# Mixing and experts in one block: first expert's weights split beside the shared output, last scores ahead of shared down, three store buffers

## The chip, the cores and the metric

The kernel runs on one core of a Trainium2 chip, as one program with one launch. The time is device time in microseconds (us); the figure that is compared is the median of a few runs. A core has TensorE (PE; its weight loads are shown as PEld), VectorE (DVE), ScalarE (ACT), GpSimd (POOL) and SyncE (SP). Each engine works through its own list in order and waits on semaphores for the others. SyncE and GpSimd also issue transfers (DMA), SyncE plain ones, GpSimd those whose rows are picked by an index.

## What is computed

One layer of a streaming encoder for 512 prompt tokens and 32 tokens of a running stream, all in f32, 1024 wide:

```
proj = x @ w_in                                 # q, k, v, z, gates, lx, ly
o    = gated_delta_rule(conv(q,k,v)) * silu(z)  # 8 heads of 128, in chunks
lru  = rg_lru(conv(lx)) * gelu(ly)
h1   = layer_norm(alpha * x + [o | lru] @ w_out)
scores = sigmoid(h1 @ router_w)                 # 64 experts in 8 groups
idx  = the 8 best experts of the 4 best groups; gw = their scores / sum * 2.5
shared = (silu(h1 @ sh_w_gate) * (h1 @ sh_w_up)) @ sh_w_down
routed = sum_j gw[j] * (silu(h1 @ w_gate[idx_j]) * (h1 @ w_up[idx_j])) @ w_down[idx_j]
y    = layer_norm(alpha * h1 + shared + routed)
```

## The kernel before

Five stages follow each other, each in a block of its own: `projection_stage`, `delta_rule_stage`, `mixing_stage`, `expert_stage`, `combine_stage`. A block ends with a barrier: each engine drains, that is, waits until what it has issued has ended, and none goes on before all have arrived. The order of the work inside a block is written out by hand for each engine. The change touches the third and the fourth stage.

`mixing_stage` multiplies by `w_out` (`mix`), turns the result to rows (`turn_mixed`), adds the residual and normalises (`normalise` on VectorE gives `h1`), turns `h1` back (`turn_h1`, copied out of PSUM by ScalarE's `copy_h1`) and computes the router's scores (`score`, L1378). The tokens come in five tiles in the order 2, 3, 4, 0, 1 (`ORDER`); tile 4 holds the 32 stream tokens. For each tile VectorE's `choose` (L1559 to L1592) finds the eight experts and writes a table of ones, `chosen` (L1585). TensorE's `ranks` (L1388) counts from it how many earlier tokens an expert has, VectorE's `place` (L1599 to L1602) turns this into a place in the list of entries, and GpSimd then writes the tile's entries there, by eight indexed transfers (L1694). When all are in memory, GpSimd reads the list of the 64 experts back (`slot_ids`, L1699) and issues the gathers of `h1` rows for the first three experts (L1183). Beside this runs the shared expert: `shared_up` (L1405, four passes of two parts), `gate` on ScalarE, `shared_hidden` on VectorE (L1621), `shared_down` for each tile (L1420), and `add_shared` on VectorE (L1631), after which SyncE stores the tile to `residual_rows`. `list_extra` and `extra_rows` (L1434) prepare a list of extra blocks for experts with over 128 tokens. SyncE has loaded the weights of the first three experts (3 MB each) since 779 us.

`expert_stage` takes the 64 experts one by one. Weights and gathered rows are split in two parts of lower precision: ScalarE writes the high part (`gate_up_hi`, L1936; `rows_hi`, L1945), VectorE the rest (`gate_up_lo`, L1993; `rows_lo`, L2002), each expert's weights in two halves. TensorE turns the rows (L1851), does 24 matmuls of gate and up (L1864 to L1866), turns the next expert's rows, does the down product of the expert before (L1884) and turns the hidden values. `write_y` on ScalarE (L1952) and VectorE (L2009) writes the weighted result to one of two buffers `y`, and GpSimd scatters them to `expert_rows` (L1802). Before `write_y(b)` both engines wait until the scatter of expert b - 2 has landed. At the stage's start ScalarE does, in this order:

```
for b in range(2):
    for u in range(2):
        split(b, u)
    if b == 0:
        read_rows(0)
```

and VectorE the same with its own parts. TensorE's first expert matmul needs `split(0, 0)` and `read_rows(0)` of both.

Of the kernel before, what the change touches and what calls it, by code (L numbers as in the profile page):

```python
# [18 lines left out]
F32 = mybir.dt.float32  # L19
BF16 = mybir.dt.bfloat16  # L20
# [1147 lines left out]
RAW = 3  # L1168
ROWS = 3
# [57 lines left out]
def mixing_stage(nc, mem, dram, route, spent):  # L1227

    with ExitStack() as ctx:  # L1229
        def sem(name):  # L1230
            return ctx.enter_context(nc.semaphore(name))

        C, PR = mem.consts, mem.params
        carve = mem.carve
        zt = carve(mem.zt, 0, DC, TW)
        lru = carve(mem.lru, 0, DC, TW)
        w_out = carve(mem.wide, 0, DC, 2 * DC, P)
        n_work = 22912
        work = mem.sbuf(ctx, "mixing_work", n_work)
        at = 0  # L1240

        def take(*dims):
            nonlocal at
            view = carve(work, at, *dims)
            at += int(np.prod(dims))
            return view

        w_gu, w_dn, w_router, ln = take(DC, 2 * FF), take(FC, D), take(DC, NE), take(2, D)
        h1 = [take(D) for _ in range(TILES + 1)]
        h1_t = take(DC, TW)  # L1250
        mixed = h1_t
        act_g, hidden_t = [take(TW - 2 * P) for _ in range(2)], take(FC, TW)
        stats, biased, masked = take(32), take(NE), take(NE)
        scores = [take(NE) for _ in range(2)]
        best, group, group_best, group_f = take(NG, 8), take(NG), take(NG), take(NG)
        group_i, top_i = take(8).bitcast(U32), take(8).bitcast(U32)
        group_eq, group_on, penalty, top_v, total = take(NG, TOPG), take(NG), take(NG), take(8), take(2)
        expert, weight, rank = take(TOPK), take(TOPK), take(TOPK)
        hot, hot_s = take(TOPK, NE), take(TOPK, NE)
        entry_f = take(TILES + 1, TOPK, 4)  # L1260
        entry = entry_f.bitcast(U32)
        dest = take(TILES + 1, TOPK).bitcast(U32)
        assert at <= n_work

        before_b, ones_b = (ctx.enter_context(nc.sbuf_tensor(n, [P, P], BF16)) for n in ("before_bf16", "ones_bf16"))

        s_w = [sem(f"w_out_loaded_{i}") for i in range(4)]
        s_sh, s_ln = sem("shared_loaded"), sem("norm_loaded")
        s_x = [sem(f"x_loaded_{t}") for t in range(TILES + 1)]
        s_copied, s_turned = sem("mix_copied"), sem("mix_turned")  # L1270
        s_mix, s_x1, s_h1, s_ht, s_htr = sem("mixed"), sem("mix_read"), sem("h1_ready"), sem("h1_transposed"), sem("h1_t_ready")
        s_scored, s_sc, s_gu, s_g, s_hid = (sem("scores_ready"), sem("scores_read"), sem("shared_up"),
                                            sem("shared_gate_ready"), sem("shared_hidden"))
        s_dn, s_acc = sem("shared_down"), sem("residual_ready")
        s_h1out = [sem(f"h1_stored_{t}") for t in range(TILES + 1)]
        s_accout = sem("residual_stored")
        s_sel, s_rank, s_placed, s_count = sem("chosen_ready"), sem("ranks_ready"), sem("entries_placed"), sem("experts_counted")
        s_extra, s_extra_row, s_v = sem("extra_blocks"), sem("extra_blocks_rows"), sem("mix_vector_steps")
        s_listed, s_ids = sem("entries_listed"), sem("slot_ids_loaded")
        block = ctx.enter_context(nc.Block())  # L1280
        tiles = token_tiles()

        def columns(t):

            return slice(tiles[t][1], tiles[t][1] + tiles[t][2])

        def group_columns(g):

            return slice(2 * P, TW - 1) if g == 0 else slice(0, 2 * P)

        def down_pair(i):

            return (4, 0, 4, 2, 0)[i]

        @block.sync
        def _(sp):
            def load_x(t):
                w = tiles[t][2]
                sp.dma_start(h1[t][0:w], dram["x_rows"][P * t:P * t + w, :]).then_inc(s_x[t], 16)

            for i, (a, b) in enumerate(zip(W_OUT_PARTS, W_OUT_PARTS[1:])):
                sp.dma_start(w_out[:, a:b], dram["w_out"][:, a:b]).then_inc(s_w[i], 16)
            load_x(ORDER[0])
            sp.dma_start(ln, dram["norms"][:, 0:2, :]).then_inc(s_ln, 16)
            sp.dma_start(w_router, dram["w_router"]).then_inc(s_sh, 16)
            load_x(ORDER[1])
            n_gu = DC * 2 * FF
            sp.dma_start(w_gu, dram["w_sh"][:, 0:n_gu].rearrange("p (k n) -> p k n", k=DC)).then_inc(s_sh, 16)
            sp.dma_start(w_dn, dram["w_sh"][:, n_gu:].rearrange("p (k n) -> p k n", k=FC)).then_inc(s_sh, 16)
            for t in ORDER[2:]:  # L1310
                load_x(t)
            def store_h1(i):
                t, w = ORDER[i], tiles[ORDER[i]][2]
                sp.wait_ge(s_h1, i + 1)
                sp.dma_start(dram["h1"][P * t:P * t + w, :], h1[t][0:w]).then_inc(s_h1out[t], 16)

            for i in range(len(GROUPS[0])):
                store_h1(i)
            sp.wait_ge(s_mix, 2 * DC)
            for b in range(RAW):  # L1320
                load_expert(sp, mem, dram, b)
            for i in range(len(GROUPS[0]), TILES + 1):
                store_h1(i)
            for i, t in enumerate(ORDER):
                w = tiles[t][2]
                sp.wait_ge(s_acc, i + 1)
                sp.dma_start(dram["residual"][P * t:P * t + w, :], h1[t][0:w]).then_inc(s_accout, 16)
            sp.wait_ge(s_accout, 16 * (TILES + 1))

        @block.tensor  # L1330
        def _(pe):
            def mix(g, d, fs):

                n, cols = DC * g + d, group_columns(g)
                if fs[0] == 0:
                    if n >= 2:
                        pe.wait_ge(s_copied, n - 1)
                    if g == 0 and d in W_OUT_PARTS:
                        pe.wait_ge(s_w[W_OUT_PARTS.index(d)], 16)
                for f in fs:  # L1340
                    last = nc.tensor.matmul(mem.bank[d % 2][:, 0:cols.stop - cols.start], w_out[:, d, f, :],
                                            (zt if f < DC else lru)[:, f % DC, cols],
                                            start=(f == 0), stop=(f == 2 * DC - 1))
                if fs[-1] == 2 * DC - 1:
                    last.then_inc(s_mix, 1)

            def turn_mixed(i):

                t, w = ORDER[i], tiles[ORDER[i]][2]
                pe.wait_ge(s_copied, DC if t in GROUPS[0] else 2 * DC)  # L1350
                if i:
                    pe.wait_ge(s_x1, i)
# [951 lines left out]
```

## Time and profile before

| | us |
|---|---|
| median of 3 runs | 1609.47 |
| lowest and highest | 1601.35, 1614.27 |
| the profiled execution: time | 1609.28 |
| its span, first to last instruction | 1607.5 |
| projection and delta rule | 0 to 646 |
| mixing, to TensorE's last matmul | 646 to 845.5 |
| first to last matmul of the experts | 864.6 to 1509.9 |
| combine | to 1607.5 |
| busy: TensorE, VectorE, ScalarE, GpSimd | 1468.6, 1009.9, 606.1, 348.8 |
| TensorE's mean granted clock | 0.952 |

The profile shows one execution. Positions in it are us from the span's start. The granted clock is a share of TensorE's full 2.4 GHz; 0.50 is its lower level, 1.2 GHz. Busy time is without semaphore, branch and DMA-issuing instructions.

### The profile page before, as it was taken

Reading aid. Unit: us, or ns where it says so; the run is one execution under the profiler, and the core shown is the slowest. Engines: PE = TensorE matmul, PEld = TensorE weight load, DVE = VectorE, ACT = ScalarE, POOL = GpSimd, SP = SyncE. Lnnn points to the kernel's source line nnn. Section 1 sums busy time; section 2 is a strip of 40 time slices with the busy share of each in tenths; the row PEclk is TensorE's granted clock in tenths of the full one; section 3 lists DMA queues with packets and bytes.
Section 4 is the critical chain, followed back from the end, with each engine's and each line's share of the span. In section 5 each row is a group of like instructions: output and inputs, shape, how many; then the busy total and the mean of one; then the engine's idle time right before and its main releaser. Section 6 shows DMA issues by size and latency. Waiting matters only on the chain. (4 is left out here: it accounts for less than half of the span.)

```text
span 1607.5 us, 21220 instructions
## 1 busy us (share of the span) xinstructions
PE 1468.6 (91%) x8256; PEld 1174.6 (73%) x8260; DVE 1009.9 (63%) x1712; ACT 606.1 (38%) x890; POOL 348.8 (22%) x233
## 2 busy tenths in 40 slices
PE   7999999979999986899995999999999999999564
PEld 5999999968888875688753667777777777777321
DVE  5649877235657665018665777777777777777277
ACT  2575333340330320001104555555555555556101
POOL 0000000022223312001441333333333223221124
PEclk9999999979999996899997999999999999999886
DMA  5212222200000000900515999999999999997392
GB/s 204 68 66 93 85 86 91 68 14 1 1 1 1 1 1 27 376 1 31 232 65 192 370 367 377 369 377 370 369 367 362 367 369 365 361 370 296 137 401 95
DMA packets 53305, 313.25 MB, mean 195 GB/s; under 512 B 14944, under 2 KB 15968, under 8 KB 34336
## 3 DMA queue, kind: packets, MB, share of 16 engines
q1 hardware_dynamic: 33456, 276.16, 45.4%
q0 software_dynamic: 19760, 35.89, 6.0%
q8 instruction: 57, 0.93, 0.2%
q14 instruction: 32, 0.26, 0.0%
HBM read 301.33 MB, written 42.12 MB: 214 GB/s over the span
## 5 line engine op out<-in xcount | busy, mean ns | idle before, releaser
L1993 DVE TENSOR_TENSOR gate_up_lo<-wide,gate_up_hi 128x2048 fp32r<-128x2048 f32 x128 | 293.0, 2290 | 101.1 <-ACT gate_up_hi L1936 99.5
L1936 ACT ACTIVATE gate_up_hi<-wide 128x2048 fp32r<-128x2048 f32 x128 | 244.6, 1913 | 29.6 <-PEq L1229 29.6
L310 PE MATMUL bank<-x_hi,w_hi 128*128 128x274 f32 x768 | 223.9, 291 | 0.0
L312 PE MATMUL bank<-x_hi,w_lo 128*128 128x274 f32 x768 | 223.0, 290 | 0.0
L311 PE MATMUL bank<-x_lo,w_hi 128*128 128x274 f32 x768 | 222.0, 289 | 0.0
L1864 PE MATMUL bank<-gate_up_hi,rows_hi 128*128 128x512 f32 x512 | 206.2, 403 | 7.1 <-DVE rows_lo L2002 7.1
L1866 PE MATMUL bank<-gate_up_hi,rows_lo 128*128 128x512 f32 x512 | 201.2, 393 | 0.0
L1865 PE MATMUL bank<-gate_up_lo,rows_hi 128*128 128x512 f32 x512 | 200.5, 392 | 0.0
L1802 POOL DMA_INDIRECT expert_rows<-lru,slot_ids x64 | 129.3, 2021 | 311.7 <-DVE lru L2009 299.3
L1884 PE MATMUL bank<-wide,zt 128*128 128x512 f32 x344 | 154.8, 593 | 1.0 <-DVE zt L2029 1.0
L310 PEld LDWEIGHTS bank<-x_hi,w_hi 128*128 128x128 f32 x768 | 144.9, 189 | 0.8 <-issue 0.5
L311 PEld LDWEIGHTS bank<-x_lo,w_hi 128*128 128x128 f32 x768 | 145.0, 189 | 0.3
L312 PEld LDWEIGHTS bank<-x_hi,w_lo 128*128 128x128 f32 x768 | 145.0, 189 | 0.0
L1864 PEld LDWEIGHTS bank<-gate_up_hi,rows_hi 128*128 128x128 f32 x512 | 96.6, 189 | 26.2 <-DVE rows_lo L2002 7.7
L1866 PEld LDWEIGHTS bank<-gate_up_hi,rows_lo 128*128 128x128 f32 x512 | 96.5, 188 | 21.1
L1865 PEld LDWEIGHTS bank<-gate_up_lo,rows_hi 128*128 128x128 f32 x512 | 96.8, 189 | 18.8
L1884 PEld LDWEIGHTS bank<-wide,zt 128*128 128x128 f32 x344 | 62.0, 190 | 62.9 <-issue 61.7
L1964 ACT ACTIVATE zt<-bank 128x256 f32<-128x256 f32 x64 | 24.6, 385 | 215.7 <-PE bank L1866 215.7
L1183 POOL DMA_INDIRECT zt<-h_rows,slot_ids x64 | 66.5, 1039 | 161.5 <-PE bank L1851 154.8
L494 DVE TENSOR_TENSOR w_lo<-w_raw,w_hi 128x1024 fp32r<-128x1024 f32 x48 | 58.7, 1224 | 56.0 <-ACT w_hi L385 54.9
L2002 DVE TENSOR_TENSOR rows_lo<-bank,rows_hi 128x512 fp32r<-128x512 f32 x128 | 82.4, 686 | 17.1 <-ACT rows_hi L1945 16.8
L991 POOL TENSOR_TENSOR delta_work<-consts,decay 128x1024 f32<-128x1024 f32 (+1 forms) x5 | 8.9, 1785 | 330.2 <-POOLq L193 330.2
(280 smaller groups left out, 2475.6 us busy)
## 6 DMA issues: line engine op xcount, KB each, us to landing
wide<-in_w_exp SPq DMA_DIRECT2D x64, 2048.0 KB
wide<-in_w_exp SPq DMA_DIRECT2D x43, 1024.0 KB
w_raw<-in_w_in SPq DMA_DIRECT2D x48, 512.0 KB, 3.5
last_down<-in_w_exp SPq DMA_DIRECT2D x21, 1024.0 KB
expert_rows<-expert_rows SPq DMA_DIRECT2D x8, 2048.0 KB, 13.5
wide<-in_w_out SPq DMA_DIRECT2D x1, 4096.0 KB, 22.0
zt<-in_x_t SPq DMA_DIRECT2D x2, 1096.0 KB, 9.3
wide<-in_w_out SPq DMA_DIRECT2D x2, 1024.0 KB, 5.9
```

Source lines behind the costliest of these rows:

```text
L310: nc.tensor.matmul(out, wh[:, k, :], x_hi[:, k, at], start=(k == 0), stop=False)
L311: nc.tensor.matmul(out, wh[:, k, :], x_lo[:, k, at], start=False, stop=False)
L312: last = nc.tensor.matmul(out, wl[:, k, :], x_hi[:, k, at], start=False, stop=(k == DC - 1))
L1183: return pool.indirect_dma_start(out=into, out_offset=None, in_=dram["h1"], in_offset=bass.IndirectOffsetOnAxis(ap=index, axis=0), bounds_ ...
L1802: return pool.indirect_dma_start(out=dram["expert_rows"], out_offset=bass.IndirectOffsetOnAxis(ap=index, axis=0), in_=source, in_offset=No ...
L1864: nc.tensor.matmul(out, x_hi[i][:, k, :], w_hi[i][:, at], start=(k == 0), stop=False)
L1865: nc.tensor.matmul(out, x_hi[i][:, k, :], w_lo[i][:, at], start=False, stop=False)
L1866: last = nc.tensor.matmul(out, x_lo[i][:, k, :], w_hi[i][:, at], start=False, stop=(k == DC - 1))
L1884: last = nc.tensor.matmul(mem.bank[4 + n][:, :], hidden_t[:, c, :], w_dn[b % RAW][:, c, 512 * n:512 * n + 512], start=(c == 0), stop=(c == ...
L1936: nc.scalar.activation(half(w_hi[b % 2], u), half(w_gu[b % RAW], u), ACT.Copy).then_inc(s_whi, 1)
L1993: nc.vector.tensor_tensor(half(w_lo[b % 2], u), half(w_gu[b % RAW], u), half(w_hi[b % 2], u), ALU.subtract).then_inc(s_wlo, 1)
L2002: nc.vector.tensor_tensor(x_lo[b % 2][:, at, :], in_fours(mem.bank[h]), x_hi[b % 2][:, at, :], ALU.subtract).then_inc(s_xlo, 1)
```

## The change

Both stages now stand in one block. Each returns one function per engine, and `mixing_and_experts` runs, on each engine, the mixing part and then the expert part, with no barrier between. What the barrier guarded is now guarded by waits: TensorE waits for the last `add_shared` before its first expert matmul, ScalarE (before its first silu) and VectorE (before its low half of expert 1's weights) wait for all residual stores. The memory of mixing is laid out so that the first expert's split weights fall on the shared gate and up weights, `h1_t` and `ln`. The first expert's weights are split in quarters, by ScalarE at the end of its mixing part and by VectorE between the last `add_shared` steps. `shared_down(0)` moves behind all `shared_up`, so that the last scores come before it, and VectorE does `place(3)` before `shared_hidden(1)` and `add_shared(0)` after `list_extra`. Three buffers `y` instead of two. Of ScalarE's and VectorE's alike changes the diff shows ScalarE's; VectorE has `split_rows(0)`, its wait, and then its halves of `split(1, u)`. The function with the five numbers is `down_pair`, the first PSUM bank of each tile's shared down.

```
+Y_ROWS = 3
 ...
-            w_gu, w_dn, w_router, ln = take(DC, 2 * FF), take(FC, D), take(DC, NE), take(2, D)
-            h1 = [take(D) for _ in range(TILES + 1)]
-            h1_t = take(DC, TW)
+    w_gu, h1_t, ln = take(DC, 2 * FF), take(DC, TW), take(2, D)
+    w_dn, w_router = take(FC, D), take(DC, NE)
 ...
+    h1 = [take(D) for _ in range(TILES + 1)]
 ...
-            return (4, 0, 4, 2, 0)[i]
+        return (4, 0, 4, 2, 4)[i]
 ...
-            sp.wait_ge(s_accout, 16 * (TILES + 1))
 ...
             turn_h1(4)
-            shared_down(0)
             score(4)
             ranks(3)
 ...
             shared_up(3, 1)
-            for i in range(1, TILES + 1):
+        for i in range(TILES + 1):
                 shared_down(i)
 ...
             gate(3)
+        act.wait_ge(s_gu, 4 * FC)
+        for q in range(4):
+            split_first(q)
 ...
             choose(3)
+        place(3)
             shared_hidden(1)
-            place(3)
             choose(4)
             shared_hidden(2)
             place(4)
-            add_shared(0)
             list_extra()
             shared_hidden(3)
-            for i in range(1, TILES + 1):
+        for i in range(TILES + 1):
                 add_shared(i)
+            if i < TILES:
+                split_first(i)
 ...
+    def split_first_hi(q):
+        if q == 0:
+            nc.scalar.wait_ge(s_gu_w[0], 16)
+        nc.scalar.activation(quarter(w_hi[0], q), quarter(w_gu[0], q), ACT.Copy).then_inc(s_whi, 1)
+
+    def split_first_lo(q):
+        nc.vector.wait_ge(s_whi, q + 1)
+        nc.vector.tensor_tensor(quarter(w_lo[0], q), quarter(w_gu[0], q), quarter(w_hi[0], q),
+                                ALU.subtract).then_inc(s_wlo, 1)
 ...
             transpose_rows(0)
+        pe.wait_ge(s_mixed_read, TILES + 1)
 ...
-            for b in range(2):
-                for u in range(2):
-                    split(b, u)
-                if b == 0:
-                    read_rows(0)
+        read_rows(0)
+        for u in range(2):
+            split(1, u)
+        act.wait_ge(s_mixed_stored, 16 * (TILES + 1))
 ...
-                if b >= 2:
-                    act.wait_ge(s_out[b % 2], 16 * (b // 2))
+            if b >= Y_ROWS:
+                act.wait_ge(s_out[b % Y_ROWS], 16 * (b // Y_ROWS))
 ...
-            mixing_stage(nc, mem, dram, route, spent)
-            expert_stage(nc, mem, dram, route)
+            mixing_and_experts(nc, mem, dram, route, spent)
```

TensorE's list from the last turn of `h1` (bank4, bank5) to the first `shared_up` of the second group, before:

```order
L1365 MATMUL bank4<-consts,mixing_work 128x128 [waits h1_t_ready,h1_ready]
L1365 MATMUL bank4<-consts,mixing_work 128x128 x3
L1365 MATMUL bank5<-consts,mixing_work 128x128 x4
L1420 MATMUL bank4<-mixing_work 128x512 [waits h1_t_ready,shared_hidden]
L1420 MATMUL bank4<-mixing_work 128x512
L1420 MATMUL bank5<-mixing_work 128x512 x2
L1378 MATMUL bank6<-mixing_work 128x64 [waits h1_t_ready,scores_read]
L1378 MATMUL bank6<-mixing_work 128x64 x7
L1388 MATMUL bank7<-chosen,ones_bf16 128x64 [waits entries_placed,chosen_ready]
L1388 MATMUL bank7<-chosen,ones_bf16 128x64 x2
L1388 MATMUL bank7<-chosen,before_bf16 128x64
L1405 MATMUL bank0<-mixing_work 128x256 [waits h1_t_ready,shared_hidden]
```

and now:

```order
L1361 MATMUL bank4<-consts,mixing_work 128x128 [waits h1_t_ready,h1_ready]
L1361 MATMUL bank4<-consts,mixing_work 128x128 x3
L1361 MATMUL bank5<-consts,mixing_work 128x128 x4
L1374 MATMUL bank6<-mixing_work 128x64 [waits h1_t_ready,scores_read]
L1374 MATMUL bank6<-mixing_work 128x64 x7
L1384 MATMUL bank7<-chosen,ones_bf16 128x64 [waits entries_placed,chosen_ready]
L1384 MATMUL bank7<-chosen,ones_bf16 128x64 x2
L1384 MATMUL bank7<-chosen,before_bf16 128x64
L1401 MATMUL bank0<-mixing_work 128x256 [waits h1_t_ready,shared_hidden]
```

The four matmuls of the first `shared_down`, into bank4 and bank5, are gone from here, and with them the wait for `shared_hidden` ahead of the scores in bank6.

TensorE's list from the last `shared_down` to the first expert's matmuls, before (`zt` holds the gathered rows):

```order
L1420 MATMUL bank0<-mixing_work 128x512 [waits residual_ready,shared_hidden]
L1420 MATMUL bank0<-mixing_work 128x512
L1420 MATMUL bank1<-mixing_work 128x512 x2
L1229 UNCONDITIONAL_BRANCH
L1840 UNCONDITIONAL_BRANCH [waits barrier_Pool_Activation_PE_DVE_SP_release]
L1851 MATMUL bank0<-consts,zt 128x128 [waits rows_gathered_0]
L1851 MATMUL bank0<-consts,zt 128x128 x3
L1851 MATMUL bank1<-consts,zt 128x128 x4
```

and now:

```order
L1416 MATMUL bank4<-mixing_work 128x512 [waits residual_ready,shared_hidden]
L1416 MATMUL bank4<-mixing_work 128x512
L1416 MATMUL bank5<-mixing_work 128x512 x2
L1866 MATMUL bank0<-consts,zt 128x128 [waits rows_gathered_0]
L1866 MATMUL bank0<-consts,zt 128x128 x3
L1866 MATMUL bank1<-consts,zt 128x128 x4
L1881 MATMUL bank2<-gate_up_hi0,rows_hi0 128x512 [waits weights_lo_ready,row_halves_lo_ready,residual_ready]
L1882 MATMUL bank2<-gate_up_lo0,rows_hi0 128x512
```

The two branches with the barrier are gone; the first turn waits for the gathered rows alone, and the wait for `residual_ready` stands at the first expert matmul.

VectorE's list from the fourth `add_shared` (out of bank2 and bank3) to the first low halves of expert 1, before:

```order
L1631 SCALAR_TENSOR_TENSOR mixing_work<-mixing_work,bank2 128x512 [waits h1_stored_0,shared_down]
L1631 SCALAR_TENSOR_TENSOR mixing_work<-mixing_work,bank3 128x512
L1631 SCALAR_TENSOR_TENSOR mixing_work<-mixing_work,bank0 128x512 [waits h1_stored_1,shared_down]
L1631 SCALAR_TENSOR_TENSOR mixing_work<-mixing_work,bank1 128x512
L1683 CAST routing<-bank7 1x128 [waits extra_blocks_rows]
L1684 CAST routing<-bank7 1x128
L1229 UNCONDITIONAL_BRANCH
L1987 UNCONDITIONAL_BRANCH [waits barrier_Pool_Activation_PE_DVE_SP_release]
L1993 TENSOR_TENSOR gate_up_lo0<-wide,gate_up_hi0 128x2048 [waits weights_hi_ready] x2
L2002 TENSOR_TENSOR rows_lo0<-bank0,rows_hi0 128x512 [waits row_halves_hi_ready]
L2002 TENSOR_TENSOR rows_lo0<-bank1,rows_hi0 128x512 [waits row_halves_hi_ready]
L1993 TENSOR_TENSOR gate_up_lo1<-wide,gate_up_hi1 128x2048 [waits weights_hi_ready] x2
```

and now, from the quarter ahead of the fourth `add_shared` on:

```order
L1789 TENSOR_TENSOR gate_up_lo0<-wide,gate_up_hi0 128x1024 [waits weights_hi_ready]
L1627 SCALAR_TENSOR_TENSOR mixing_work<-mixing_work,bank2 128x512 [waits h1_stored_0,shared_down]
L1627 SCALAR_TENSOR_TENSOR mixing_work<-mixing_work,bank3 128x512
L1789 TENSOR_TENSOR gate_up_lo0<-wide,gate_up_hi0 128x1024 [waits weights_hi_ready]
L1627 SCALAR_TENSOR_TENSOR mixing_work<-mixing_work,bank4 128x512 [waits h1_stored_1,shared_down]
L1627 SCALAR_TENSOR_TENSOR mixing_work<-mixing_work,bank5 128x512
L1680 CAST routing<-bank7 1x128 [waits extra_blocks_rows]
L1681 CAST routing<-bank7 1x128
L2017 TENSOR_TENSOR rows_lo0<-bank0,rows_hi0 128x512 [waits row_halves_hi_ready]
L2017 TENSOR_TENSOR rows_lo0<-bank1,rows_hi0 128x512 [waits row_halves_hi_ready]
L2008 TENSOR_TENSOR gate_up_lo1<-wide,gate_up_hi1 128x2048 [waits weights_hi_ready,residual_stored]
L2008 TENSOR_TENSOR gate_up_lo1<-wide,gate_up_hi1 128x2048 [waits weights_hi_ready]
```

The weights' low quarters (128x1024) stand between the adds, the low halves of the rows come directly after mixing, and the first low half of expert 1 waits for `residual_stored`.

## Rows read from the trace of the kernel before

**Rows 1.** Busy time by stretches: us, each engine (count), clock, DMA share, GB/s.

```profile
846.00:865.00 19.00, 2.37 (x9) 2.00 (x10) 7.37 (x9) 8.12 (x6) 5.69 (x4) 0.54 0.33 102
...
885.00:1100.00 215.00, 215.00 (x903) 151.28 (x902) 155.16 (x151) 119.70 (x127) 77.03 (x43) 1.00 0.97 373
```

**Rows 2.** One operation of VectorE, once per expert: durations ns, first and last start.

```profile
L2021 DVE TENSOR_TENSOR zt<-zt,bank x64: 413/422/422, 872.4 to 1502.0; 128x256 f32<-128x256 f32 x64
```

**Rows 3.** Timeline from the barrier's opening; columns: start, us, what, [idle before <-releaser].

```profile
856.62 1.94 PE L1851 MATMUL bank<-consts,zt 128*128 128x128 f32 x8 [11.14 <-PEq L1229]
...
856.88 3.71 ACT L1936 ACTIVATE gate_up_hi<-wide 128x2048 fp32r<-128x2048 f32 x2 [29.58 <-PEq L1229]
...
860.50 1.07 ACT L1945 ACTIVATE rows_hi<-bank 128x512 fp32r<-128x512 f32 x2
...
863.24 1.28 DVE L2002 TENSOR_TENSOR rows_lo<-bank,rows_hi 128x512 fp32r<-128x512 f32 x2
...
864.57 0.79 PE L1864 MATMUL bank<-gate_up_hi,rows_hi 128*128 128x512 f32 x1 [6.01 <-DVE rows_lo L2002]
```

**Rows 4.** One line's instructions: drains that end the mixing block, ns and start us.

```profile
L1229 POOLq DRAIN  x1: 8456/8456/8456, 847.9 to 847.9; - x1
...
L1229 SPq DRAIN  x1: 7/7/7, 849.6 to 849.6; - x1
```

**Rows 5.** Timeline of the last scatters, the last shared down and the first gather.

```profile
831.45 0.97 POOL L1694 DMA_INDIRECT slot_table<-mixing_work  x1 [2.30 <-DVE mixing_work L1602]
...
841.25 0.60 PE L1434 MATMUL bank<-consts,routing 128*1 128x128 f32 x4
...
841.78 3.70 PE L1420 MATMUL bank<-mixing_work 128*128 128x512 f32 x8
...
842.80 0.60 POOL L1699 DMA_DIRECT2D slot_ids<-slot_table  x1 [1.43 <-DMA slot_table<-mixing_work]
...
845.52 1.28 DVE L1631 SCALAR_TENSOR_TENSOR mixing_work<-mixing_work,bank 128x512 f32<-128x512 f32 x2 [2.87 <-PE bank L1420]
...
847.05 1.06 POOL L1183 DMA_INDIRECT zt<-h_rows,slot_ids  x1 [3.66 <-DMA slot_ids<-slot_table]
```

**Rows 6.** Timeline from three passes of shared up to the last placing.

```profile
816.27 10.61 PE L1405 MATMUL bank<-mixing_work 128*128 128x256 f32 x48
...
818.13 0.20 DVE L1559 TENSOR_SCALAR mixing_work<-mixing_work 128x64 f32<-128x64 f32 x1
...
824.27 0.20 DVE L1585 CAST chosen<-mixing_work 128x64 bf16<-128x64 f32 x1
...
829.04 0.69 DVE L1599 TENSOR_TENSOR mixing_work<-mixing_work,bank 128x512 f32<-128x512 f32 x1 [2.00 <-remote]
...
830.49 0.17 DVE L1602 SCALAR_TENSOR_TENSOR mixing_work<-mixing_work 128x8 uint32<-128x8 f32 x1
```

**Rows 7.** DMA queue of the gathers, 848.5 to 851: packets, MB, share.

```profile
q0 software_dynamic: 150, 0.34, 55.1%
```

**Rows 8.** Timeline before the last scores.

```profile
805.25 1.08 ACT L1502 ACTIVATE mixing_work<-bank 128x512 f32<-128x512 f32 x2 [4.62 <-PE bank L1365]
...
808.68 0.46 DVE L1621 TENSOR_TENSOR mixing_work<-mixing_work,bank 128x291 f32<-128x291 f32 x1
...
809.19 5.40 PE L1420 MATMUL bank<-mixing_work 128*128 128x512 f32 x8 [3.98 <-DVE mixing_work L1621]
...
814.43 1.89 PE L1378 MATMUL bank<-mixing_work 128*128 128x64 f32 x16
```

**Rows 9.** The page's group of the weights' low halves.

```profile
L1993 DVE TENSOR_TENSOR gate_up_lo<-wide,gate_up_hi 128x2048 fp32r<-128x2048 f32 x128 | 293.0, 2290 | 101.1 <-ACT gate_up_hi L1936 99.5
```

**Rows 10.** Timeline of a scatter that started inside an operation of VectorE.

```profile
794.30 1.28 DVE L1216 SCALAR_TENSOR_TENSOR mixing_work<-mixing_work 128x1024 f32<-128x1024 f32 x1
...
794.57 1.76 POOL L1694 DMA_INDIRECT slot_table<-mixing_work  x1 [0.30 <-issue]
```

**Rows 11.** Waits of 864 to 1515 us: total us, times, longest us.

```profile
ACT lru L1952 <- DMA expert_rows<-lru,slot_ids: 56.9, 35, 2.8
```

More of the change, by code:

```diff
@@ L1301, in _ @@
[L1301 to L1308, printed above, removed]
@@ L1320, in _ @@
[L1320 to L1327, printed above, removed]
-            sp.wait_ge(s_accout, 16 * (TILES + 1))
+            mixing["sync"](sp)
+            experts["sync"](sp)
@@ L1330, in _ @@
         @block.tensor
         def _(pe):
[L1332 to L1345, printed above, removed]
@@ L1472, in _ @@
-            shared_up(1, 1)
-            turn_h1(4)
-            shared_down(0)
-            score(4)
-            ranks(3)
-            shared_up(2, 0)
-            shared_up(2, 1)
-            shared_up(3, 0)
-            ranks(4)
-            count()
-            shared_up(3, 1)
-            for i in range(1, TILES + 1):
-                shared_down(i)
-                if i == 3:
-                    extra_rows()
+            mixing["tensor"](pe)
+            experts["tensor"](pe)
         @block.scalar
@@ L1540, in _ @@
-            copy_h1(4)
-            scored(4)
-            gate(2)
-            gate(3)
+            mixing["scalar"](act, experts["first_hi"])
+            experts["scalar"](act)
         @block.vector
         def _(dve):
-            steps = Steps(dve, s_v)
-            nc.vector.tensor_copy(before_b[:, :], C("before"))
-            nc.vector.tensor_copy(ones_b[:, :], C("ones"))
-            steps.link(nc.vector.memset(route.chosen, 0.0))
-            steps.link(nc.vector.tensor_copy(entry.rearrange("p t j c -> p (t j c)"), C("entries")))
@@ L1606, in normalise @@
-            def normalise(i):
-                t, w = ORDER[i], tiles[ORDER[i]][2]
-                dve.wait_ge(s_x[t], 16)
-                dve.wait_ge(s_turned, i + 1)
-                for n in range(2):
-                    half = h1[t][0:w, 512 * n:512 * n + 512]
-                    last = nc.vector.scalar_tensor_tensor(half, half, ALPHA, mem.bank[2 + n][0:w, :], ALU.mult, ALU.add)
-                last.then_inc(s_x1, 1)
-                dve.wait_ge(s_x1, i + 1)
-                layer_norm(nc, steps, h1[t][0:w], stats[0:w], ln[0:w, 0, :], ln[0:w, 1, :]).then_inc(s_h1, 1)
@@ L1678, in _ @@
[L1678 to L1684 removed]
+            mixing["vector"](dve, experts["first_lo"])
+            experts["vector"](dve)
         @block.gpsimd
         def _(pool):
[L1688 removed]
@@ L2049, in combine_stage @@
+            mixing["gpsimd"](pool)
+            experts["gpsimd"](pool)
 def combine_stage(nc, mem, dram, route):
```

1344 lines of the change are left out of this document (710 added, 634 removed).

## The prediction

> **What bounds the kernel now.** I read first the busy table by stretches [rows 1]. From 885 us on TensorE is busy 215.00 of 215 us, at a granted clock of 1.00: the expert loop is TensorE's. Its 64 experts follow each other evenly; the first multiply of gate and up starts at 872.4 and the last at 1502.0 [rows 2], so one expert takes (1502.0 - 872.4) / 63 = 9.99 us. No wait of TensorE stands in the list of waits of that loop. Time can be had only where TensorE is idle, and the stretch 846 to 865 is that place: 2.37 us busy in 19.00, clock 0.54 [rows 1].
>
> I then read the timeline of that stretch backwards, from TensorE's first expert matmul at 864.57 [rows 3]. It waited for the low half of the gathered rows (VectorE, 863.24), this for their high half (ScalarE, 860.50), and this stood behind 3.71 us of splitting the first weights, which began at 856.88, although the weights had long been in memory. Everything begins at 856.6, when the barrier between the two blocks opens. The engines' drain rows [rows 4] say who was late: SyncE arrived at 849.6, while GpSimd's drain of 8.456 us ran from 847.9 to 856.4. So GpSimd closes the block, after it has issued the three first gathers. What leads to them [rows 5]: the list entries of the last token tile are placed at 830.49 + 0.17 = 830.66 [rows 6], eight scatters run 831.45 to 841.37, the list is read back (842.80), the first gather starts at 847.05. Its rows were there about 850.9: by 851 the gathers had moved 150 packets [rows 7], a little more than the 128 rows of the first one.
>
> **The change, part by part.**
>
> (a) The last scores go ahead of shared down. Today TensorE ends the last turn of h1 at 805.21, then waits 3.98 us for shared_hidden(1), which VectorE gives only after choose(3), and then does the eight matmuls of shared_down(0) in 5.40 us; the same eight take 3.70 at full clock, so the idling cost 1.7 more. The last scores come at 814.43 [rows 8]. Afterwards they need only ScalarE's copy, done at 806.33: they start about 806.4, end at 808.2, and the ranks of tile 3 follow, whose choice is on hand before 806.7. VectorE, free at 808.64 (808.68 is its next start), places tile 3 at once: 1.62 us (829.04 to 830.66, [rows 6]), to 810.35; with shared_hidden(1), 0.46, it is at 810.9. choose(4) now starts there and not at 818.13. Its chosen table comes 6.34 us later (818.13 to 824.47), at 817.2, and its end (one 512-wide product and one sum of 0.69 each, three small steps) about 2.1 after that, 819.3. TensorE's three shared_up passes take 10.6 us from 808.3 [rows 6], to 818.8: they, not VectorE, release the last ranks, at 819.0. shared_hidden(2) and place(4) take 0.45 + 1.62: entries placed at 821.4 instead of 830.66, **9.2 us earlier**. GpSimd's backlog doesn't eat this: tile 3 is placed 810.35, its eight scatters take 0.8 + 9.9 us as the last tile's do now, to 821.0.
>
> (b) TensorE's own end of mixing. After the ranks: shared_up(3,1), 3.5, to 822.5; five shared_down of 3.43 each (8 matmuls at 0.43) and 0.54 for the extra rows (841.25 to 841.78, [rows 5]) give 840.2, against 841.78 + 3.70 = 845.5 now. VectorE's last add follows to 841.5. So TensorE is free 5 us earlier and no longer the later of the two.
>
> (c) The first weights' splits move under shared down. 3.71 us of ScalarE and 4.5 of VectorE leave the entrance. ScalarE has been idle there for 29.6 us [rows 3], so its four quarters (3.71 us in all) cost nothing. VectorE's quarters (half of 2290 ns, 1.15 us each, [rows 9]) lie between add_shared steps: one add takes 1.28, one shared_down 3.43, which leaves 1.0 us; if that cover were gone each would delay the next add. But GpSimd issues its scatters at the same time. When a scatter started at 794.57 inside VectorE's 1.28 us operation on two operands of mixing_work, it took 1.76 us [rows 10] where others take 0.97 [rows 5]; it ended 0.75 after VectorE did. A quarter of 1.15 against scatters every 1.28 catches nearly always one start, and delays it by 0 to 1.15, on average 0.5. The first quarter can start at 822.5 + 3.43 + 1.28 = 827.2, the next each one shared_down later. Two quarters (827.2, 830.6) fall into the scatters of the last tile, a third (834.1) on the list's read-back, the fourth (837.5) ends before the gather: 0.5 + 0.5 + 0.4 = **1.4 us lost**, ends 0 and 3.5. [...]
>
> (d) The barrier goes. First gather: placed 821.4, + 0.8 to GpSimd's start, + 9.9 for eight scatters [rows 5], + 1.4 (c), + 1.43 until the entries have landed, + 4.25 (842.80 to 847.05) = 839.2; rows about 3.85 after the start (847.05 to 850.9) = 843.0. TensorE, free since 840.2, turns them. From the turn's start to the first expert matmul: 1.94 for both halves at half clock, ScalarE's second half 0.54, VectorE's 0.64, hand-overs 0.1 = 3.2 us. First matmul at 846.2 instead of 864.57: **18.4 us saved**. I take half clock, since TensorE idles 2.8 us beforehand and the 3.98 us of today brought it down.
>
> (e) New waits. Before the second expert's low weights VectorE waits for all residual stores. Behind this are queued the split of expert 1 and the first hidden product. The last store is issued at 841.6 and landed in some 2.4 us in the trace (SyncE is at its drain 849.6 after the add's end at 846.8 [rows 4, 5]): 844.2, before VectorE has finished the rows (846.1). The split ends about 850.9, its first half by 848.6, while TensorE needs that first half at about 854 (8 us after its first matmul). Zero, with 5 us of cover. ScalarE's same wait stands before its first silu, at 853: zero. TensorE's wait for the last add (841.5): zero.
>
> (f) Three store buffers. ScalarE waits in the loop 35 times, 56.9 us in all, for the store of two experts ago [rows 11]. It had spare time: 119.70 busy in 215 us, and TensorE was at 215.00 of 215. Zero; bounds +1 and -1 us.
>
> Sum against the profiled execution: 1609.28 - 18.4 = 1590.9 us. That execution lies 0.2 us under the median of the three runs, 1609.47, so the forecast is **1591 us**.
>
> **Rivals.**
> 1. A late slot. TensorE idles 1.2 us before the moved scores (805.2 to 806.4). If its clock falls there, three shared_up passes lose some 1.7 us as shared_down(0) did [rows 8], the last ranks and all behind them come as much later; if each quarter holds a scatter in full besides, 2.1 more. 18.4 - 3.8 = 14.6: 1594.9. For it: the clock did fall in this neighbourhood. Against: after a gap three times as long.
> 2. All falls well: no scatter is held (1.4), and after an idle time of only 1.4 us TensorE keeps its clock, which gives the turn 0.9 less and the first expert 1.7 less. 22.4: 1587.1.
> 3. Something not in the trace (code that has to be fetched, a store or gather that lands late among the new loads) takes 6 to 13 us of the entrance back: about 1600. Then the new wait for the stores (e) is the last one; it decides from a landing 5 us later than I have.
> 4. **Slower.** The third buffer lets ScalarE run ahead, splits end up to 2.8 us earlier and weight loads are issued earlier, among the stores. DMA is at 0.97 from 885 to 1100 [rows 1]. If loads and gathers get in each other's way until TensorE waits for weights, the loop's period rises; the gain is gone at 18.4 / 63 = 0.29 us more per expert, and at 0.8 more (10.8 us) the kernel takes 1591 + 50 = 1641. For it: 0.97, and the 35 waits for stores. Against: the same bytes in the same time, and from 885 to 1100 TensorE never waited.
> 5. The change doesn't do what it says: GpSimd's gathers would still stand behind a barrier. The order shows none, so I give it nothing.
>
> **How the numbers follow.** Forecast (saving 16 to 20.5) 0.55; rival 1 0.20; rival 2 0.16; rival 3 0.06; rival 4 0.03. Savings of 14 to 22.5 us hold 0.9 of this and are 1587 to 1595.5; runs of the kernel before lie 8.1 under and 4.8 over their median, so a median of a few runs may stand 4 to 5 off: 1582 to 1600. A measurement of this kernel can tell about 1%, 16.1 us, from no change: the line is 1593.4, only 2.4 over the forecast. The whole forecast case and rival 2 lie under it, but the scatter of runs takes some of it away: faster 0.61, within 1% 0.36, slower 0.03.
>
> **What the profile afterwards would show.** Last scores near 806 and entries placed near 821 (a); no drain between mixing and experts, four weight quarters of 1.15 us among the last adds, and scatters of over 1.3 us beside them (c); first gather near 839, first expert matmul near 846 (d); VectorE's split of expert 1 done before 852 (e); the loop still 9.99 to 10.03 per expert with no wait of ScalarE for stores (f). It is wrong if the first gather starts after 843, if TensorE waits inside the loop, or if its end of mixing comes after the rows.

## The result and the profile after

The changed kernel takes 1593.39 us (median of 8 runs, 1591.85 to 1594.98), the kernel before 1610.12 beside it (8 runs); the ratio is 0.9895, 95% interval 0.9878 to 0.9911: faster by 1.05%. Forecast were 1591.0 and 1582 to 1600; the measured median lies on the line, 1593.4, that the prediction drew for 1%. The profiled execution took 1594.97, its span is 1593.2.

Since whole executions shift against each other before the place of the change (the last turn of h1 starts at 804.17 in the trace before and between 803.8 and 807.4 in the later ones), I write +x for times from that start, 805.85 in this trace. The timeline of the changed kernel at the entrance (start, us, what, [idle before <-releaser]):

```profile
808.15 1.97 PE L1374 MATMUL bank<-mixing_work 128*128 128x64 f32 x16 [1.26 <-ACT mixing_work L1496]
...
823.42 0.97 POOL L1690 DMA_INDIRECT slot_table<-mixing_work  x1 [0.30 <-issue]
...
829.18 1.22 DVE L1789 TENSOR_TENSOR gate_up_lo<-wide,gate_up_hi 128x1024 fp32r<-128x1024 f32 x1
829.81 1.43 POOL L1690 DMA_INDIRECT slot_table<-mixing_work  x1 [0.30 <-issue]
...
832.61 1.22 DVE L1789 TENSOR_TENSOR gate_up_lo<-wide,gate_up_hi 128x1024 fp32r<-128x1024 f32 x1
832.83 1.85 POOL L1690 DMA_INDIRECT slot_table<-mixing_work  x1 [0.30 <-issue]
836.11 0.60 POOL L1695 DMA_DIRECT2D slot_ids<-slot_table  x1 [1.43 <-DMA slot_table<-mixing_work]
...
839.71 1.06 POOL L1184 DMA_INDIRECT zt<-h_rows,slot_ids  x1 [3.00 <-DMA slot_ids<-slot_table]
...
844.07 0.32 SPq L1325 DMA_DIRECT2D residual_rows<-mixing_work  x1
844.43 0.43 SPq L1796 DMA_DIRECT2D wide<-in_w_exp  x1
845.49 1.37 PE L1866 MATMUL bank<-consts,zt 128*128 128x128 f32 x8 [2.77 <-DMA zt<-h_rows,slot_ids]
...
848.32 0.77 PE L1881 MATMUL bank<-gate_up_hi,rows_hi 128*128 128x512 f32 x1 [1.46 <-issue]
...
849.97 2.29 DVE L2008 TENSOR_TENSOR gate_up_lo<-wide,gate_up_hi 128x2048 fp32r<-128x2048 f32 x1 [1.75 <-DMA residual_rows<-mixing_work]
```

The last scores stand at 808.15, +2.30, where they were at 814.43, +10.26 [rows 8]. The first gather is at +33.9 (before 847.05, +42.9 [rows 5]), and the rows are turned as soon as they land, with no barrier between [rows 3]. The first expert matmul is at +42.47; before at 864.57, +60.40: 17.9 us less. The busy table by stretches (us, each engine, clock, DMA share, GB/s) answers [rows 1], and by two us it shows the clock:

```profile
846.00:865.00 19.00, 16.40 (x71) 12.96 (x70) 12.55 (x11) 10.31 (x11) 1.98 (x2) 0.82 0.74 282
885.00:1100.00 215.00, 215.00 (x899) 149.95 (x898) 154.24 (x151) 123.22 (x131) 75.62 (x43) 1.00 0.97 372
...
845.00:847.00 2.00, 1.37 (x8) 0.97 (x8) 0.19 (x1) 0.70 (x2) 0.00 (x0) 0.79 1.06 303
847.00:849.00 2.00, 0.68 (x2) 0.61 (x3) 1.19 (x2) 2.00 (x2) 0.99 (x1) 0.50 0.92 365
849.00:851.00 2.00, 2.00 (x6) 1.54 (x5) 1.03 (x1) 2.00 (x2) 0.00 (x0) 0.50 0.99 418
851.00:853.00 2.00, 2.00 (x6) 1.59 (x5) 2.00 (x2) 0.09 (x1) 0.00 (x0) 0.50 0.84 348
853.00:855.00 2.00, 2.00 (x10) 1.63 (x10) 1.46 (x1) 0.00 (x0) 0.00 (x0) 1.00 0.47 195
```

TensorE is busy 16.40 of 19 us where it was 2.37. But it waited 2.77 us for the rows and 1.46 for their halves, and its granted clock is 0.50 until 853: the first expert runs mostly at 1.2 GHz. The operation of [rows 2] now runs from 856.7 to 1486.3, 629.6 us as before. The spans differ by 14.3 us: entrance 17.9, less 1.7 (the last turn of h1 came later), 0.5 (first expert), 0.4 (exit) and 1.0 (final combine).

### The profile page after: what moved, and what is told of

It reads as the page before. It is cut to its first block and busy times, and to the rows that moved or that the text cites. A ratio compares the mean times of both kernels' runs of the same rounds, so it can differ in the third digit from the quotient of the medians.

```text
span 1593.2 us, 21215 instructions
## 1 busy us (share of the span) xinstructions
PE 1473.6 (92%) x8256; PEld 1180.0 (74%) x8260; DVE 1004.6 (63%) x1714; ACT 602.5 (38%) x892; POOL 377.7 (24%) x233
## 5 line engine op out<-in xcount | busy, mean ns | idle before, releaser
L2008 DVE TENSOR_TENSOR gate_up_lo<-wide,gate_up_hi 128x2048 fp32r<-128x2048 f32 x126 | 288.0, 2287 | 63.7 <-ACT gate_up_hi L1953 61.9
L1818 POOL DMA_INDIRECT expert_rows<-lru,slot_ids x64 | 157.1, 2455 | 302.8 <-DVE lru L2024 291.6
L2035 DVE TENSOR_TENSOR zt<-zt,bank 128x256 f32<-128x256 f32 x64 | 27.0, 421 | 101.7 <-ACT zt L1980 101.7
## 6 DMA issues: line engine op xcount, KB each, us to landing
last_down<-in_w_exp SPq DMA_DIRECT2D x21, 1024.0 KB, 14.3
expert_rows<-expert_rows SPq DMA_DIRECT2D x8, 2048.0 KB, 14.3
```

What stands on the lines that cost most here:

```text
L1818: return pool.indirect_dma_start(out=dram["expert_rows"], out_offset=bass.IndirectOffsetOnAxis(ap=index, axis=0), in_=source, in_offset=No ...
L2008: nc.vector.tensor_tensor(half(w_lo[b % 2], u), half(w_gu[b % RAW], u), half(w_hi[b % 2], u), ALU.subtract).then_inc(s_wlo, 1)
```

## The experiments

Each ratio is against the kernel before, beside it on the same chip. The point +0 is an event of TensorE, and it moves against VectorE's work by what TensorE's clock was just before. The busy tables of the `shared_up` matmuls ahead of `score(3)`, the last scores but one, first in the changed kernel, then in the one whose fourth residual store is held (further below); the third number from the end is the granted clock:

```profile
794.43:800.14 5.71, 5.71 (x16) 4.17 (x17) 5.15 (x19) 0.00 (x0) 4.49 (x5) 0.70 1.02 428
...
796.37:800.39 4.02, 4.02 (x17) 3.14 (x17) 3.74 (x11) 0.00 (x0) 3.10 (x4) 1.00 1.02 428
```

Nine of the thirteen traces have a mean granted clock of 0.70 there, the before and the changed one among them; four have 1.00: scores moved back, scores alone, the held store and the held load. In these four TensorE arrives earlier, so all of VectorE's and GpSimd's work stands 0.8 to 0.9 us later in +x (entries placed at +17.6 and not +16.7 in three of them) without any edit having caused it. Why the clock differed stays open.

**The barrier back** (two blocks again, with SyncE's wait for the stores at the end of the first; the rest as changed).

```
+        sp.wait_ge(s_accout, 16 * (TILES + 1))
```

> The changed kernel with the barrier put back between its two parts; all else as changed (quarters of the first weights among the adds, last scores ahead, three buffers). Measured from the start of the last turn of h1 to the first expert matmul, the kernel before needs 60.4 us and the changed one 42.5. Theory (the chain over GpSimd sets the entrance; the barrier waits for GpSimd's drain, which ended 9.35 us after the first gather's start before): first gather 33.9 us after the last turn as in the changed kernel, drain over at 43.2, rows turned from 43.4, first matmul at 46.6, so 4.1 us lost: 1597.5 us. Rival (the splits alone were what the barrier held, the drain would end with the rows): first matmul at most 1 us later, 1594. Rival (the barrier is the whole gain): first matmul at 55 or later, over 1606.

1599.58 us, 0.9929 (0.9902 to 0.9956). Timeline of its entrance:

```profile
842.34 0.32 SPq L1325 DMA_DIRECT2D residual_rows<-mixing_work  x1
848.60 1.94 PE L1867 MATMUL bank<-consts,zt 128*128 128x128 f32 x8 [7.62 <-PEq L2074]
```

The first gather stayed at +33.8, and TensorE waited 7.62 us for the barrier; first expert matmul +47.9, so 5.4 us later. It opened 10.7 us after the gather, not 9.35, which is most of the 1.3 us that the expectation missed. Seen from this side the barrier is worth 5.4 us of trace and 6.2 of the medians.

**The scores moved back.**

```
         turn_h1(4)
+        shared_down(0)
         score(4)
```

> The changed kernel with its first part undone: shared_down(0) ahead of the last scores again, place(3) behind shared_hidden(1), add_shared(0) ahead of list_extra; the four quarters of the first weights follow the adds 1, 2 and 3 (two behind the last). Theory (a chain: last scores, choose, place, scatters, list, gather, rows): the last entries are placed 26.5 us after the last turn of h1 as before and not 16.5, everything behind is 8 to 9 us later, first expert matmul 51 us after that turn instead of 42.5: 1602 us. Rival (TensorE's own end of mixing sets the entrance, GpSimd has slack): first matmul 45 to 46, 1597 us.

1606.96 us, 0.9978 (0.9962 to 0.9993): 13.6 over the changed kernel, not 8.6. Two things in its timeline were not in my sum:

```profile
810.82 6.58 PE L1416 MATMUL bank<-mixing_work 128*128 128x512 f32 x8 [4.91 <-DVE mixing_work L1618]
817.23 1.89 PE L1374 MATMUL bank<-mixing_work 128*128 128x64 f32 x16
...
849.60 1.06 POOL L1184 DMA_INDIRECT zt<-h_rows,slot_ids  x1 [3.79 <-DMA slot_ids<-slot_table]
...
850.00 0.43 SPq L1800 DMA_DIRECT2D wide<-in_w_exp  x1
...
859.71 1.97 PE L1870 MATMUL bank<-consts,zt 128*128 128x128 f32 x8 [11.42 <-DMA zt<-h_rows,slot_ids]
```

The eight matmuls ran after an idle time of 4.91 us with the clock granted at 0.50 and took 6.58 us (3.70 in [rows 5], 5.40 after a gap of 3.98 in [rows 8]). And the rows landed 10 us after the gather. The 2 MB load of the fourth expert's weights is issued 0.4 us after it. In the kernel before it came at 863.35: the barrier had kept it back, and behind the barrier the split of the first weights, whose buffer it fills.

**The same, with that load held until the first rows are there.**

```
+                if b == RAW - 2:
+                    sp.wait_ge(s_rows[0], 16)
```

> The kernel with the last scores put back behind shared down, and with one more wait: the 2 MB load of the fourth expert's weights, which SP issues 0.4 us after the first gather there, waits until the first gather's rows have landed. Theory A (the 10 us from gather to rows there were the load's packets in front of the rows): rows at most 5.7 us after the gather, as in the changed kernel, so first expert matmul at +54 instead of +58.3 from the start of the last turn of h1, and a time of 1602.7 us, 4.2 under the same kernel without the wait. Theory B (the landing is long for another reason, such as the gather's own descriptors or TensorE's half clock): rows 10 us after the gather still, +58.3, 1607 us.

1600.93 us, 0.9933 (0.9913 to 0.9952): 6.0 us less by one wait.

```profile
848.13 1.06 POOL L1184 DMA_INDIRECT zt<-h_rows,slot_ids  x1 [3.80 <-DMA slot_ids<-slot_table]
...
853.29 0.33 SPq L1802 DMA_DIRECT2D wide<-in_w_exp  x1
853.32 1.97 PE L1872 MATMUL bank<-consts,zt 128*128 128x128 f32 x8 [6.53 <-DMA zt<-h_rows,slot_ids]
```

Rows 5.2 us after the gather instead of 10.1: theory A. The other 2.1 us by which its first expert matmul is earlier, +51.26 against +58.26, are not the wait's doing: 0.93 is the shift of +0 told above, which is also the gap of 3.98 instead of 4.91, and 1.18 is the eight matmuls behind it, 5.40 instead of 6.58.

**The scores alone** (the kernel before, its barrier kept, with the last scores first).

```
-            shared_down(0)
             score(4)
```

> The kernel before with one part of the change alone: last scores ahead of shared_down(0), place(3) ahead of shared_hidden(1), add_shared(0) behind list_extra. Two blocks, the first weights split behind the barrier, two buffers. Theory (the chain over GpSimd leads to the barrier too): entries placed 10 us earlier, first gather 32.6 us after the last turn of h1 (42.9 before), drain over at 42, first expert matmul 50.2 instead of 60.4: 10 us saved, 1600 us beside 1610. Rival (TensorE's end of mixing or the residual stores close the block then): TensorE ends at 36.6, stores at 41, so these would give the same barrier only if the drain ended before 41; first matmul at 49. Rival (VectorE's last adds, now later, take it back): under 5 us saved.

1602.58 us, 0.9947 (0.9930 to 0.9965): 8.2 us. First gather 9.0 earlier, at +33.9; but the barrier opened 10.8 us after it instead of 9.6, so 7.8 arrive (both 0.9 more, by the shift of +0). Scores alone 8.2 and barrier 6.2 make 14.4 of the 16.7 together. What lies between these two kernels is the first weights' splits beside shared down, and the third buffer, which brings nothing (below): by the ratios 0.9947 and 0.9929 it is 0.18%, 2.9 us, though their intervals overlap. Taken the other way round, barrier removed and splits moved with the scores left late bring 3.3, because the load then gets in front of the rows, and 9.9 with that load held.

**The quarters after the adds.**

```
             add_shared(i)
-            if i < TILES:
-                split_first(i)
+        for q in range(4):
+            split_first(q)
```

> The changed kernel with VectorE's four quarters of the first weights moved behind the last add_shared. Theory (a scatter that starts inside such a quarter is held until it ends): the last tile's eight scatters take 9.9 us from first start to last end and not 11.3, the first gather starts 1.3 us earlier, at 32.6 us after the last turn of h1; but VectorE then has 4.9 us of quarters behind the last add (38.2), so the rows' low half comes at 44.4 and the first expert matmul at 44.5 instead of 42.5: 1595.4 us. Rival (nothing holds scatters, 11.3 us is GpSimd's own pace in this stretch): scatters 11.3 us and gather at 33.9 as in the changed kernel, first matmul 44.5 too.

1595.34 us, 0.9899 (0.9874 to 0.9925). Timeline, last scatters:

```profile
832.57 0.97 POOL L1690 DMA_INDIRECT slot_table<-mixing_work  x1 [0.30 <-issue]
833.85 0.97 POOL L1690 DMA_INDIRECT slot_table<-mixing_work  x1 [0.30 <-issue]
834.24 3.86 SPq L1325 DMA_DIRECT2D residual_rows<-mixing_work  x2
837.34 0.59 POOL L1695 DMA_DIRECT2D slot_ids<-slot_table  x1 [2.52 <-DMA slot_table<-mixing_work]
```

The last tile's eight scatters now all take 0.97: the quarters did hold them. They end 1.4 us earlier from the last turn of h1, at +27.5, but the entries landed 2.52 us afterwards instead of 1.43: the read-back comes only 0.3 us sooner. That is not because a held scatter is free. In the kernel before [rows 5], and in the one with the held store, where the last scatter is not held either, the read-back starts 2.40 us after that scatter's start:

```profile
835.23 0.97 POOL L1692 DMA_INDIRECT slot_table<-mixing_work  x1 [0.30 <-issue]
837.63 0.59 POOL L1697 DMA_DIRECT2D slot_ids<-slot_table  x1 [1.43 <-DMA slot_table<-mixing_work]
```

In the changed kernel it is 3.28, and the difference is the 0.88 for which the scatter was held. Late quarters has 3.49 with nothing held. There a 512 KB store is issued at 834.24, while the last scatter runs (833.85 to 834.82), and the DMA engines are 0.91 busy from 835.0 to 836.5; in the changed kernel that store's packets were over at about the held scatter's end. So the earlier entries most likely waited behind the store; no run moved that store to show it. The first expert matmul was +44.4, 1.9 later, because the splits then stand at the entrance.

**Two store buffers** (`Y_ROWS = 2`).

> The changed kernel with two store buffers. Theory (ScalarE waits in time that it has to spare, TensorE sets the loop's period): ScalarE waits some 50 us in all for stores of two experts ago, the loop's period stays 10.02 us, time within 1 us of the changed kernel, 1593.4. Rival (the third buffer holds up part of the gain): each wait costs TensorE 0.1 us or more, 1600 us.

1593.72 us, 0.9894 (0.9871 to 0.9918). ScalarE waits for stores again:

```profile
ACT lru L1969 <- DMA expert_rows<-lru,slot_ids: 99.1, 40, 4.7
```

The loop took 630.1 us against 629.6. The third buffer removes waits that cost nothing.

**TensorE kept busy** (26 dummy transposes into an unused corner of PSUM, 16 ahead of the turn of the rows, 10 behind it).

```
+        keep_busy(16)
         transpose_rows(0)
+        keep_busy(10)
```

> The changed kernel, with 16 transposes of the identity into an unused corner of PSUM ahead of the turn of the first rows and 10 behind it, whose results nobody reads. Theory (TensorE's clock falls to 0.50 because it idles 2.8 us and 1.5 us there, and stays down until 852.9): the clock stays at 1.00 through the first expert, whose 24 matmuls take 5.6 us and not 7.7, so 2.1 us saved: 1591.3 us. Rival (the fall comes from something else, such as the whole activity before): clock at 0.50 as before and the added transposes delay the first matmul by up to 1 us: 1594.

1590.51 us, 0.9880 (0.9857 to 0.9903), the lowest of all. Timeline of its entrance:

```profile
843.09 1.09 PE L1866 MATMUL bank<-consts,zt 128*128 128x128 f32 x8 [0.65 <-DMA zt<-h_rows,slot_ids]
...
845.80 0.47 PE L1881 MATMUL bank<-gate_up_hi,rows_hi 128*128 128x512 f32 x1 [0.53 <-issue]
```

Its busy table by stretches:

```profile
843.00:845.00 2.00, 1.92 (x18) 1.92 (x18) 0.59 (x1) 1.22 (x3) 0.05 (x1) 1.00 0.99 299
845.00:847.00 2.00, 1.47 (x8) 1.08 (x7) 0.70 (x2) 2.00 (x2) 0.94 (x1) 1.00 1.13 432
847.00:849.00 2.00, 2.00 (x10) 1.63 (x9) 1.42 (x1) 1.47 (x1) 0.00 (x0) 1.00 0.96 403
```

The clock stays at 1.00, and from the first expert's first matmul to its gate it is 5.8 us instead of 8.0; the second expert's gate comes 2.7 us earlier, at +55.9. The medians differ by 2.9 us, and the slowest of its 5 runs (1591.65) lies under the fastest of the changed kernel's 8 (1591.85), though the two were not measured side by side and the intervals of their ratios overlap.

**Stores and load against the rows.** Three kernels: the fourth residual store held until the first rows have landed; that with the dummy transposes; and the changed kernel with only the fourth expert's load held, by the two lines shown above.

```
             sp.wait_ge(s_acc, i + 1)
+            if i == 3:
+                sp.wait_ge(mem.rows_gathered[0], 16)
```

> The changed kernel, with SyncE holding the fourth residual store until the first gathered rows have landed. Theory (the first gather, issued at 839.71 in the changed kernel's trace, waited behind the fourth store's 512 KB, issued at 839.91, whose packets ran until 842): rows land 3.8 us after the gather's start and not 5.7, the first expert matmul comes 1.9 us earlier, 40.6 us after the last turn of h1: 1591.5 us. Two stores then land among the new loads; VectorE's wait for them may last until 851, still ahead of the need at 857. Rival (the gather's 5.7 us is GpSimd's own: writing of descriptors): no change of the landing, same time. Rival (the late stores hold VectorE's split of expert 1 too long): second expert late, slower by 1 us or more.

> Both additions at once. Theory: the rows land about 1 us after TensorE's last shared_down, the 16 transposes (2.1 us) then stand ahead of the turn and cost 1 us, the clock stays at 1.00: 3 us saved against the changed kernel, 1590.4 us. Rival: only the larger of the two gains, 1591.5.

> The changed kernel with the same wait on its load of the fourth expert's weights, which it issues at 844.43, 4.7 us after the first gather and 1.1 before the rows are turned. Theory A: the load came too late to be in front of the rows, so rows are turned at +39.6 as before (0.3 either way), the last residual store lands earlier by up to 3 us because it no longer shares with the load, and VectorE starts expert 1's split at +42 to +43 instead of +44.1; none of it is on the path: 1593.4 us, no change. Rival: the load's first packets did delay the rows; then the rows are turned at +38 to +39 and the time is 1592 us.

They took 1594.68 (0.9894), 1594.33 (0.9898) and 1595.22 us (0.9901, 0.9884 to 0.9918): the medians show no gain (single runs of the first two go from 1589.2 to 1595.7, so a gain of 1 us could hide). Holding the store does bring the rows earlier: with the dummy transposes in both, they were turned at +38.45 instead of +39.26, the gather being at +33.7 in both. Of the load alone I can't say it: the rows were turned at +39.5, as theory A has it, but 4.7 us after a gather that had come 0.9 late. In the first and third kernel all entries were placed at +17.6 instead of +16.7, the shift of +0. In the second the first expert's gate was 0.9 us earlier than with the dummy transposes alone, but the second expert's 3.5 later, at +59.5. VectorE waited 3.7 us for the late stores, and its lateness reached TensorE, which stood idle 1.91 us before turning the first hidden values and 0.76 more before the second expert:

```profile
854.63 0.44 PE L1893 MATMUL bank<-consts,zt 128*128 128x128 f32 x2 [1.91 <-DVE zt L2043]
855.83 0.79 PE L1883 MATMUL bank<-gate_up_hi,rows_hi 128*128 128x512 f32 x1 [0.76 <-DVE rows_lo L2025]
...
857.00:859.00 2.00, 2.00 (x7) 1.51 (x6) 2.00 (x3) 0.01 (x1) 0.00 (x0) 0.50 0.98 422
```

The second expert's first matmul was only 0.6 us later than with the dummy transposes alone (+50.77 against +50.14). The other 2.9 us are the clock: it fell to 0.50, and from that matmul to the gate it took 8.7 us instead of 5.8.

**And the load held until the stores have landed**, on top of the second of these.

```
+                if b == RAW - 2:
+                    sp.wait_ge(s_mixed_stored, 16 * (TILES + 1))
```

> The changed kernel with the dummy transposes, the fourth residual store held until the first rows have landed, and the load of the fourth expert's weights held until all residual stores have landed. Without the last wait the second expert came late because VectorE waited 3.7 us for the stores. Theory A (the stores were late because the 2 MB load shared the DMA engines with them): they now land about 2.5 us sooner, expert 1's split starts at +42.5 instead of +44.7, second expert's gate at +55.2 instead of +59.5, rows turned at +38.5: 1589.6 us, 0.9 under the kernel with the dummy transposes alone. Rival (a store of 512 KB takes its time whatever shares with it, so holding it costs what the rows gain): second gate at +56 or later, 1591 us or more.

1595.13 us, 0.9901 (0.9886 to 0.9917). Timeline of VectorE:

```profile
849.89 4.49 DVE L2018 TENSOR_TENSOR gate_up_lo<-wide,gate_up_hi 128x2048 fp32r<-128x2048 f32 x2 [3.86 <-DMA residual_rows<-mixing_work]
```

Its DMA issues from 843.5 to 845.5 (KB each, us to landing):

```profile
residual_rows<-mixing_work SPq DMA_DIRECT2D x1, 512.0 KB, 6.4
zt<-h_rows,slot_ids POOLq DMA_INDIRECT x1, 5.8
```

Without any load a residual store still took 6.4 us, so the load didn't make it late, and the time went the rival's way. What did stays open: the two stores of 512 KB were issued together, at 843.06 to 843.86, and the gathers ran beside them. In TensorE's rows the clock falls to 0.50 for the second expert here too (2.04 us idle, then 0.76).

## Why the forecast held, and where it was off

The steps bore out in this order. (a) Scores +2.30 (forecast +2.2), entries placed +16.7 (+17.2). GpSimd came straight from tile 3's scatters, with 0.30 us between, so its backlog, which I had called harmless, and the placing tie: the last tile's scatters began 0.9 us after it. (b) TensorE's end of mixing was +36.9, forecast +36.0; not on the path.

(c) I charged 1.4 us for held scatters. Two were held, 0.46 and 0.88 us, each until 0.85 us after VectorE's operation, 1.34 in all, and all of it delayed the entries. So the cost was sized rightly. That late quarters brought back only 0.3 us of it is most likely the work of the store that its entries then met. A scatter that started inside an add, whose second input comes from PSUM, was not held (831.55, 0.97 us, inside the add at 831.41). The Trainium skill, page "SBUF — State Buffer", section "SBUF: two separate sides", says that a VectorE instruction with two SBUF inputs contends with a GpSimd instruction that reads SBUF, and these rows agree. It also reports that `tensor_tensor` was not seen to stall a DMA; here a `tensor_tensor` of two SBUF operands held one (1.43 and 1.85 us instead of 0.97), and the measurement decides.

(d) The first gather was at +33.9, forecast +35.0: the entries were placed 0.5 us earlier and the read-back took 3.60 us, not 4.25. The rows then took 5.8 us, not 3.85. This is the term that was mis-sized, and mostly by how I read it: 3.85 was never a landing, but the time until the three gathers together had moved 150 packets [rows 7]. Counted in the same way, from 839.7 to 844.0, the changed kernel had

```profile
q0 software_dynamic: 144, 0.32, 30.7%
```

that is 4.3 us after its gather's start, and yet the rows were turned only at 845.49. With the load held (scores moved back) 138 packets had moved after 4.0 us and the rows came after 5.2. So some 1.2 to 1.5 us lie between such a count and the landing, and only 0.4 to 0.7 us is left for a difference in the traffic. Nor was the old trace free of traffic: there too a store of 512 KB was issued beside the gather of 847.05.

```profile
846.83 0.32 SPq L1327 DMA_DIRECT2D residual_rows<-mixing_work  x1
```

What traffic can do is shown by the held store (with the dummy transposes the rows were turned 4.8 us after the gather, and 5.6 without the hold) and by the load just behind the gather (10.1 us). The turn to the first matmul took 2.8 us, not 3.2. The errors nearly cancel, gather 1.1 early, rows 1.9 late, turn 0.4 short: 17.9 us saved against 18.4. That the sum came so close is in part luck. The sum left out the first expert's multiplies at half clock (0.5) and could not foresee exit and combine (1.4).

(e) The last store landed about 849.9, not 844.2, so VectorE's split of expert 1 ended at 854.5 and not before 852, a sign that I had named and that failed. Still it cost nothing: its first half was ready at 852.3, and TensorE reached the second expert at 858.66. With the store held and the dummy transposes in, the wait did reach TensorE and cost 3.5 us, most of it by the clock. (f) Nothing, as two buffers showed.

Rival 1 is out: after the gap of 1.26 us before the scores the granted clock was still 1.00, and it fell in the traces with 3.98 and 4.91 us. Rival 2 did not occur, since TensorE idled 2.8 us and not 1.4; but it had priced the kept clock at 0.9 and 1.7 us, and the dummy transposes, which kept it, were worth 2.7 us at the second gate. Rival 3's mechanism is real, though it did not decide here: the late landing took 6 us as soon as the scores were late. Rival 4: loop and DMA share unchanged.

## What to carry to other kernels

When a barrier goes, ask what it had held back: here a 2 MB load which, issued beside a small gather on the critical path, makes the gather take 10 us instead of 5. (That is the variant with late scores; in the changed kernel the load came 4.7 us after the gather.) Price a transfer by what will share the DMA engines with it at its new time, and by a wait that ended on it, not by a count of packets. A cost that one order shows, such as the held scatters, is not what the other order gives back: something else may then stand in front. And where the bound engine idles a few us before its long stretch, cheap filler work can pay twice, in the first operations too, but look at which wait its haste uncovers, and whether the clock falls again there. When times are counted from an event of one engine, check that engine's clock just before it.

## What the hardware showed that I had not expected

A VectorE subtraction of two SBUF operands held a GpSimd scatter until 0.85 us after its own end, and the scatter's entries landed later by all that it was held: 2.40 us from its start to the read-back when free, 3.28 when held for 0.88. The same gather of 128 rows took 4.5 to 4.7 us to land with the store or the load beside it held, 5.2 to 5.8 with a store of 512 KB beside it, and 10.1 with a load of 2 MB issued 0.4 us behind it. A gap of 1.91 and 0.76 us with two short matmuls between them was followed by a granted clock of 0.50, while the one gap of 1.26 us before the last scores left it at 1.00.
